# Expert stages of a two-block transformer: the first block's transposed rows as a product with a one-hot of positions

## The reference

```
def hier_moe(xf, w_rg, b_rg, w_re, b_re, w1, w3, w2):      # T rows of 1024
    ...                                  # router: best group of 4, in it the 2 best of 8 experts
    expert = g_idx * EXPERTS_PER_GROUP + top_i             # two experts for each token
    gate = jax.nn.softmax(top_v, axis=-1) * g_val
    ...                                  # the rows are sorted by expert and padded to blocks
    def expert_block(args):
        xblk, e = args
        return (jax.nn.silu(xblk @ w1[e]) * (xblk @ w3[e])) @ w2[e]
    yb = lax.map(expert_block, (xb, block_exp)).reshape(R, D)
    out = jnp.zeros((T + 1, D), yb.dtype).at[row_tok].add(yb * row_gate[:, None])
    return out[:T]
```

## Time and profile before

| | us |
|---|---|
| median of 3 runs (lowest, highest) | 2503.63 (2503.33, 2508.33) |
| the profiled execution | 2508.48 |
| its span | 2506.6 |
| PE busy in the span | 2295.7 (92%) |
| DVE, ACT, POOL busy | 1279.3, 689.4, 120.4 |

### The profile page before, as it was taken

The page is one execution under the profiler, slowest core; times in us unless marked ns, Lnnn a source line. Parts: engine busy times, 40 slices in busy tenths (PEclk is TensorE's granted clock), DMA queues, the critical chain, the costliest instruction groups (busy, mean ns, idle before and its releaser), DMA issues.

```text
span 2506.6 us, 37162 instructions
## 1 busy us (share of the span) xinstructions
PE 2295.7 (92%) x14742; PEld 1606.3 (64%) x14742; DVE 1279.3 (51%) x2026; ACT 689.4 (28%) x941; POOL 120.4 (5%) x219
## 2 busy tenths in 40 slices
PE   8999999989999999999948999999888779988887
PEld 7888788889888788888743444433485634333333
DVE  5556655565556655562564665555678532111112
ACT  4334543343334543342211011000146301100110
POOL 1000100000001000000001000000000010000000
PEclk9999999999999999999978999999989889999999
DMA  9774437757765287743267999999931479999997
GB/s 329 250 255 148 146 125 262 258 163 245 246 233 167 76 284 245 257 131 101 77 244 286 404 406 408 407 407 408 355 114 51 163 315 409 413 411 412 415 417 308
DMA packets 235391, 673.59 MB, mean 269 GB/s; under 512 B 23920, under 2 KB 163456, under 8 KB 181888
## 3 DMA queue, kind: packets, MB, share of 16 engines
q1 hardware_dynamic: 213584, 642.82, 68.6%
q0 software_dynamic: 9584, 17.52, 2.4%
q10 hardware_dynamic: 12096, 11.48, 1.5%
HBM read 675.62 MB, written 4.29 MB: 271 GB/s over the span
## 4 chain that ended last, share of the span: by engine, by line
PE 68%; DMA 19%; DVE 7%; DVEq 2%; ACT 2%; issue 2%; SPq 0%; ACTq 0%; POOLq 0%
PE ps L708 14%; PE ps L709 14%; PE ps L710 13%; DMA raw<-in_w 12%; PE ps L1155 11%; DMA expert_ahead<-in_w 7%; PE ps L1173 4%; PE ps L1226 2%; PE ps L722 2%; PE ps L749 2%; DVE w_lo L1912 1%; PE ps L1148 1%; DMA router_rows<-work 1%; PE ps L1165 1%; PE ps L1366 1%
## 5 line engine op out<-in xcount | busy, mean ns | idle before, releaser
L1912 DVE TENSOR_TENSOR w_lo<-raw,w_hi 128x2048 fp32r<-128x2048 f32 x180 | 411.1, 2289 | 318.0 <-ACT w_hi L1416 317.4
L708 PE MATMUL ps<-t_hi,w_hi 128*128 128x256 f32 (+1 forms) x1568 | 454.4, 290 | 0.1
L709 PE MATMUL ps<-t_lo,w_hi 128*128 128x256 f32 (+1 forms) x1568 | 452.6, 289 | 0.0
L1416 ACT CAST w_hi<-raw 128x2048 fp32r<-128x2048 f32 x180 | 342.1, 1905 | 394.9 <-PE ps L710 381.3
L710 PE MATMUL ps<-t_hi,w_lo 128*128 128x256 f32 (+1 forms) x1568 | 449.7, 287 | 0.0
L708 PE MATMUL ps<-w_hi,t_hi 128*128 128x256 f32 (+1 forms) x1088 | 352.2, 324 | 10.1 <-DVE t_lo L1912 7.9
L709 PE MATMUL ps<-w_lo,t_hi 128*128 128x256 f32 (+1 forms) x1088 | 351.3, 323 | 0.0
L710 PE MATMUL ps<-w_hi,t_lo 128*128 128x256 f32 (+1 forms) x1088 | 351.2, 323 | 0.0
L708 PEld LDWEIGHTS ps<-t_hi,w_hi 128*128 128x128 f32 x1568 | 295.0, 188 | 20.1 <-issue 13.2
L2624 DVE SCALAR_TENSOR_TENSOR work<-ps,work 128x512 f32<-128x512 f32 x64 | 48.1, 751 | 501.1 <-PE ps L1173 501.0
L710 PEld LDWEIGHTS ps<-t_hi,w_lo 128*128 128x128 f32 x1568 | 296.0, 189 | 4.6
(11 more groups left out here) (352 smaller groups left out, 2563.8 us busy)
## 6 DMA issues: line engine op xcount, KB each, us to landing
expert_ahead<-in_w SPq DMA_DIRECT2D x188, 1024.0 KB, 24.3
raw<-in_w SPq DMA_DIRECT2D x128, 1024.0 KB, 24.1
work<-in_w SPq DMA_DIRECT2D x60, 1024.0 KB, 26.4
work<-in_w_mod SPq DMA_DIRECT2D x32, 1536.0 KB, 6.5
raw<-in_ffn_w_gate SPq DMA_DIRECT2D x44, 1024.0 KB, 8.9
raw<-in_ffn_w_up SPq DMA_DIRECT2D x44, 1024.0 KB, 10.6
raw<-in_ffn_w_down SPq DMA_DIRECT2D x44, 1024.0 KB, 4.9
raw<-in_w_in SPq DMA_DIRECT2D x18, 1024.0 KB, 5.3
```

The lines of the kernel that those rows point to most:

```text
L708: pe.matmul(dst, a[0], b[0], start=start, stop=False)
L709: pe.matmul(dst, a[0], b[1], start=False, stop=False)
L1416: act.copy(slot(j)[0], src).then_inc(w_hi_ready, 1)
L1912: return dve.tensor_tensor(dst, src, hi.bitcast(F32), ALU.subtract)
```

## The change

For block 0 of each stage the rows are no longer gathered from DRAM and transposed. DVE makes a one-hot of position within expert 0 for every token (`r_first`), and PE multiplies the normed rows in SBUF with it (`first_rows`): the product is the transposed block. It goes to the same bank and through the same copy to `xT`, which moves to another place in the work area, since `hrow` still fills the old one when m = 0.

The main table (block = expert, 32 columns) is made at once, from positions alone. The spare blocks are worked out after it, and their columns come with the second table. Gather 0 is gone; gather 1 is the first. Gathers with a fixed block number read their addresses from `table` directly, with no copy and no drain. For m = 0, ACT's first copy to `gusb` now also waits for `h_stored`.

```
-                slot_table(1, 2)
-                pe.wait_ge(table_ready, m + 1)
+                def first_rows():
+                    pe.wait_ge(first_ready, m + 1)
+                    pe.wait_ge(rows_ready, TILES[0] * m + nt)
+                    for kk in range(KD):
+                        for t in range(nt):
+                            mm = pe.matmul(ps[:, 0, kk * BLK:(kk + 1) * BLK], hrow[:, t, :].rearrange("p (c k) -> p k c", k=KD)[:, kk, :],
+                                           r_first[:, t, :], start=t == 0, stop=t == nt - 1)
+                    mm.then_inc(xgt_ready, 1)
+
+                first_rows()
+                slot_table(1, 2, r_main_onehot, EXPERTS)
...
-                turn_rows(0, 0)
                 up_of(0, 0)
                 turn_rows(1, 1)
-                slot_table(2, 4)
+                pe.wait_ge(table_ready, m + 1)
+                slot_table(2, 4, r_onehot, nb + EXTRA[m])
                 turn_up(0, 0)
...
                 dve.wait_ge(pos_ready, m + 1)
+                pos_ps = ps[:, 1, 0:nt * 32].rearrange("p (t n) -> p t n", t=nt)
+                first = r_first[:, 0:nt, :]
+                wide = lambda v: v.to_broadcast([P, nt, BLK])
+                dve.tensor_tensor(first, iota[:, 0:BLK].unsqueeze(1).to_broadcast([P, nt, BLK]), wide(pos_ps[:, :, 0:1]), ALU.is_equal)
+                dve.drain()
+                dve.tensor_tensor(first, first, wide(r_mem[:, 0:nt, 0:1]), ALU.mult)
+                dve.drain().then_inc(first_ready, 1)
...
+                dve.tensor_tensor(blocks[:, :, :, 0:EXPERTS], r_oh[:, :, 0:nt, :], bk(tokid[:, :, 0:nt], EXPERTS), ALU.mult)
...
+                dve.tensor_tensor(chosen, r_oh[:, :, 0:nt, :], pos_ps.unsqueeze(1).to_broadcast([P, 2, nt, EXPERTS]), ALU.mult)
+                dve.drain()
+                dve.tensor_reduce(r_pos[:, :, 0:nt], chosen, X, ALU.add)
+                dve.drain()
+                dve.tensor_tensor(main, slots, bk(r_pos[:, :, 0:nt], BLK), ALU.is_equal)
+                dve.drain().then_inc(onehot_ready, 1)
+
+                dve.wait_ge(tps_ready, 2 * m + 1)
+                dve.tensor_scalar(table[0:BLK, 0:EXPERTS], ps[0:BLK, 2, 0:EXPERTS], 1.0, 4.0 * BANK, ALU.mult, ALU.add)
+                dve.tensor_scalar(token_f[:, 0:EXPERTS], ps[:, 2, 0:EXPERTS], 1.0, 4.0 * BANK, ALU.mult, ALU.add)
+                dve.drain().then_inc(table_ready, 1)
+
                 more = r_more[:, :, 0:2 * nt - 1]
...
-                for par in range(2):
-                    dve.wait_ge(xg_landed[m][par], 16)
-                block_onehots(gates)
+                onehots = r_onehot[:, 0:2 * nt, :].rearrange("p (k t) n -> p k t n", k=2)
+                is_blk = r_is_blk[:, 0:2 * nt, 0:nb].rearrange("p (k t) n -> p k t n", k=2)
+                dve.tensor_tensor(onehots, slots, bk(r_inf[:, :, 0:nt], BLK), ALU.is_equal)
...
+                dve.tensor_tensor(blocks[:, :, :, 0:nb], is_blk, bk(gates[:, :, 0:nt], nb), ALU.mult)
+                dve.tensor_tensor(blocks[:, :, :, nb:nb + nx], is_blk[:, :, :, EXPERTS:nb], bk(tokid[:, :, 0:nt], nx), ALU.mult)
+                dve.drain().then_inc(onehot_ready, 1)
...
+                    if isinstance(b, int):
+                        rows = table[0:BLK, b:b + 1]
...
-                gather(0, 0, True)
                 gather(1, 1, True)
```

More of the change, by code:

```diff
@@ L350, in build @@
         r_more = r(2592, EXPERTS, 7)
-        r_blk = r(2816, 8, 48)
+        r_blk = r(2816, 8, 64)
+        r_is_blk = r(1952, 8, 48)
+        r_pos = w(R2 + 2576, 8).rearrange("p (k t) -> p k t", k=2)
+        r_main_onehot = r(1440, 8, BLK)
+        r_first = w(R1 + 1040, 4 * BLK).rearrange("p (t n) -> p t n", t=4)
         r_onehot = r(256, 8, BLK)
@@ L455, in build @@
         onehot_ready = sem("slot_onehots_ready")
+        first_ready = sem("first_block_onehot_ready")
         tps_ready = sem("table_product_ready")
@@ L1135, in slot_table @@
                         for half in range(2):
[L1136 removed]
+                            mm = pe.matmul(ps[BLK * half:BLK * half + BLK, bank, 0:n], onehot[:, i, :], r_blk[:, i, 0:n],
                                            start=i == 0, stop=i == 2 * nt - 1)
                     mm.then_inc(tps_ready, 1)
[L1140 to L1141 removed]
+                def first_rows():
[8 more added lines that the diff above has]
+                slot_table(1, 2, r_main_onehot, EXPERTS)
                 def turn(par):
@@ L1770, in up_copy @@
                     act.wait_ge(expert_done, MAIN * m + (6 * b + 2 if not isinstance(b, int) or b else 4))
+                    if m == 0 and isinstance(b, int) and b == 0:
+                        act.wait_ge(h_stored, 64)
                     act.copy(gusb[:, par, :], ps[:, 1, :]).then_inc(gu_ready, 1)
@@ L2498, in moe @@
                 dve.wait_ge(pos_ready, m + 1)
+                pos_ps = ps[:, 1, 0:nt * 32].rearrange("p (t n) -> p t n", t=nt)
[5 more added lines that the diff above has]
+                dve.drain().then_inc(first_ready, 1)
                 pos = r_tmp[:, 0:nt, :]
-                dve.tensor_copy(pos, ps[:, 1, 0:nt * 32].rearrange("p (t n) -> p t n", t=nt))
+                dve.tensor_copy(pos, pos_ps)
                 dve.tensor_copy(r_cnt, ps[:, 1, nt * 32:nt * 32 + 32])
-                dve.drain()
+                tokid = k("tokid").rearrange("p (k t) -> p k t", k=2)
+                blocks = r_blk[:, 0:2 * nt, :].rearrange("p (k t) n -> p k t n", k=2)
+                bk = lambda v, n: v.unsqueeze(3).to_broadcast([P, 2, nt, n])
+                dve.tensor_tensor(blocks[:, :, :, 0:EXPERTS], r_oh[:, :, 0:nt, :], bk(tokid[:, :, 0:nt], EXPERTS), ALU.mult)
+                chosen = r_chosen[:, :, 0:nt, :]
+                main = r_main_onehot[:, 0:2 * nt, :].rearrange("p (k t) n -> p k t n", k=2)
+                slots = iota[:, 0:BLK].unsqueeze(1).unsqueeze(1).to_broadcast([P, 2, nt, BLK])
+                dve.tensor_tensor(chosen, r_oh[:, :, 0:nt, :], pos_ps.unsqueeze(1).to_broadcast([P, 2, nt, EXPERTS]), ALU.mult)
+                dve.drain()
+                dve.tensor_reduce(r_pos[:, :, 0:nt], chosen, X, ALU.add)
[6 more added lines that the diff above has]
+                dve.drain().then_inc(table_ready, 1)
                 more = r_more[:, :, 0:2 * nt - 1]
@@ L2542, in moe @@
                 dve.drain()
-                tokid = k("tokid").rearrange("p (k t) -> p k t", k=2)
-                def block_onehots(value):
-                    for kk in range(2):
-                        for t in range(nt):
-                            dve.tensor_scalar(r_blk[:, kk * nt + t, 0:nb], iota[:, 0:nb], r_blkf[:, kk, t:t + 1],
-                                              value[:, kk, t:t + 1], ALU.is_equal, ALU.mult)
-                    dve.drain().then_inc(onehot_ready, 1)
-                onehots = r_onehot[:, 0:2 * nt, :].rearrange("p (k t) n -> p k t n", k=2)
-                dve.tensor_tensor(onehots, iota[:, 0:BLK].unsqueeze(1).unsqueeze(1).to_broadcast([P, 2, nt, BLK]),
-                                  r_inf[:, :, 0:nt].unsqueeze(3).to_broadcast([P, 2, nt, BLK]), ALU.is_equal)
-                block_onehots(tokid)
                 dve.wait_ge(route_exp_ready, 2 * m + 1)
@@ L2588, in moe @@
                 dve.tensor_copy(extra_used[0:1, m:m + 1], incl[0:1, EXPERTS - 1:EXPERTS])
+                dve.wait_ge(tps_ready, 2 * m + 2)
+                dve.tensor_scalar(table[0:BLK, EXPERTS:nb], ps[0:BLK, 4, nb:nb + nx], 1.0, 4.0 * BANK, ALU.mult, ALU.add)
+                dve.tensor_scalar(token_f[:, EXPERTS:nb], ps[:, 4, nb:nb + nx], 1.0, 4.0 * BANK, ALU.mult, ALU.add)
                 dve.drain().then_inc(extra_ready, 1)
@@ L2823, in rows_in @@
                 def rows_in(b, par):
-                    pool.tensor_copy(table_col[0:BLK, par:par + 1], table[0:BLK, bass.ds(b, 1)])
-                    pool.drain()
+                    if isinstance(b, int):
+                        rows = table[0:BLK, b:b + 1]
+                    else:
+                        rows = table_col[0:BLK, par:par + 1]
+                        pool.tensor_copy(rows, table[0:BLK, bass.ds(b, 1)])
+                        pool.drain()
                     return pool.indirect_dma_start(out=xg[0:BLK, par, :], out_offset=None, in_=h_dram,
-                                                   in_offset=bass.IndirectOffsetOnAxis(ap=table_col[0:BLK, par:par + 1], axis=0),
+                                                   in_offset=bass.IndirectOffsetOnAxis(ap=rows, axis=0),
                                                    bounds_check=nt * P - 1, oob_is_err=False)
```

19 lines of the change are left out of this document (7 added, 12 removed).

## The result

| | us |
|---|---|
| median of 5 runs (lowest, highest) | 2489.3 (2488.61, 2493.57) |
| kernel before, median of 5 runs beside them | 2505.16 (2503.33, 2508.86) |
| ratio, 95% interval | 0.9938 (0.9923, 0.9952) |
| the profiled execution, its span | 2490.68, 2488.9 |

The changed kernel is 15.9 us faster (0.62%), inside the range of 2474 to 2492 and 7 us short of the forecast of 2482.

A forecast was written before the change was run, and what follows sets the result against it. Weights bound the long expert run, which could only start earlier, by as much as PE's work at the stage starts shrank. Gains of 8.8 (m = 0) and 12.5 us (m = 1), 21.3 together, gave a median of 2482, range 2474 to 2492.

The forecast's parts named there:

- The rule that the end moves by PE's work on blocks 1 to 3: Stage starts: the program's end moves as much as PE's work on these blocks, while DMA has a pause to give up.
- Rival 3: Stage starts: the head start is worth nothing because the weights bind and DMA regains its pause; 2503.6 us, chance 0.06.
- The new product at 0.12 a record: Block 0's one-hot product on PE: 64 records in 7.7 us for m = 0, 32 in 3.8 for m = 1.
- The clock rising during the product: PE, m = 0: dense work raises the clock after 3 to 4 us, so the first table takes 1.1 us, not 1.95.
- The hole of 7.2 us left with the first indirect transfer: POOL, m = 0: the one-time 7.2 us delay stays ahead of gather 1, which starts at about 1317.3.
- rival 2: POOL: the 7.2 us hole belongs to the copy and drain and falls on gather 2; 2475 us, chance 0.12.
- m = 1, 12.5 us forecast: Second stage start: block 1's up product ends at 2030.3 against 2042.85, with no PE idling and no clock lost.
- `h_stored` last in m = 0: Gather 1's release: the row store at 1309.58 comes after the table at 1309.4, so the store is last.
- DVE in time, DMA in time: Second one-hots ready 3.9 us before PE asks in m = 0; weight panels arrive before block 3 asks, so nothing eats the gain.
- rival 1: New product: loads and products don't overlap, 0.2 us a record, 12.8 and 6.4 us; 2490 us, chance 0.15.
- Rival 4: New product: records run unpipelined, only ground the accumulation in one place of PSUM; slower, 2516 us, chance 0.04.
- Rival 5: One stage's gain is halved by the clock in m = 1's block 0, late one-hots or slow gather 1; 2490 us, chance 0.07.

The follow-up runs named there:

- e8: Changed kernel with twelve extra matmuls ahead of the product to keep the clock up, and a plain contiguous stationary; 2479.9 us, 0.9898 of the kernel before.
- e12: Changed kernel with the extra clock-raising matmuls and a stationary stride of two elements (8 bytes) in place of eight; 2480.56 us (one time).
- e6: Changed kernel with eight extra matmuls while PE waited for the membership and four more ahead of the product, to raise the clock; 2491.2 us, 0.9948 of the kernel before.
- e11: Changed kernel with the extra clock-raising matmuls and both operands of the product cut to 64 partitions; 2494.59 us (one time).
- e9: Changed kernel with the extra clock-raising matmuls, product loops exchanged and no sums over the tiles; 2492.39 us (one time).
- e4: Changed kernel with the product's operands exchanged: one-hot stationary, rows moving 512 columns at a time, result then turned; 2478.39 us, 0.9894 of the kernel before.
- e1: Changed kernel with the product's stationary read from neighbouring columns in place of every eighth; 2489.23 us, 0.9938 of the kernel before.
- e3: Changed kernel with the copy of the table's column and the drain put back ahead of gather 1; 2500.95 us, 0.9982 of the kernel before.
- e5: Kernel before with only gathers 0 and 1 reading addresses directly from the table, no copy or drain; 2498.7 us, 0.9978 of the kernel before.
- e2: Changed kernel with the product for block 0 taking only the first tile of tokens, 16 records per stage; 2481.4 us, 0.9905 of the kernel before.

## Why the prediction was right or wrong

- **The rule that the end moves by PE's work on blocks 1 to 3**: right. Block 1's up product and SP's transfers moved by the same 8.3 us, and the weight-bound run kept its length. Over all the kernels the stage starts differ by up to 26.5 us, and what comes after them by 1.3. Rival 3 falls.
- **The new product at 0.12 a record: the step that failed.** It took the price from L1148, with the same stride and 64 moving columns. The product has 0.242 a record, 15.5 and 7.9 us for 7.7 and 3.8, above even the bound of 13.6, which came from a plain stationary at half clock. e8 and e12 show the forecast's size (0.124 and 0.127) once the stride is short and the clock up; e6 shows 0.24 with the long stride at full clock. The row of the right kind was L722, a float32 matmul like the new product: its 0.21 and 0.11 at half and full clock are what the plain product costs in e8 (0.213 and 0.112), and only the price of the stride was in no such row. Why the transposes of L1148 get by with 0.14 and less for one record of the same stride is open: hardly for their 64 partitions (e11), and not for having no sum (e9). They are one record for an operation of the code where a float32 matmul is two, and no run parts these. One row points the same way: the turning in e4 (L1164) is made of float32 matmuls with this stride, of 64 columns, on the two halves of the partitions side by side. Its 16 records for each half take 2.13 us, 0.13 each, which is about half of 0.24 for half the columns.
- **The clock rising during the product**: wrong. I took L722's dense work as the pattern; L1151 is as dense in the profile and the clock stayed at 0.50 for 15.3 us. The stride isn't the whole reason: in e1 the clock stayed at 0.50 too, for the 13.9 us of the plain product. Why it rose in L722 and in e4 and not here is open. So the first table (1.92 for 1.1 in m = 0) and the first 5 us of `up_of(0)`, in both stages, ran at half clock.
- **The hole of 7.2 us left with the first indirect transfer**: wrong. It follows the first copy (rival 2; e3, e5). The forecast read a hole of 8.05 us and later ones of 0.89; the two gathers between them had 2.79 and 2.50. Because the hole went elsewhere the errors nearly cancelled in m = 0, and that is luck. From start to start, the product was 7.7 us too long, the table 0.6 and `up_of(0)` 2.6, 10.9 together. Against it stand the 5.8 us of idling, the 2.0 of lost clock and 1.2 in the transposes, second table and `turn_up` that I had counted behind the late gather, 9.0 together. So 1.9 us were missing, and 2.0 were measured (6.8 for 8.8).
- **m = 1, 12.5 us forecast, 6.9 measured**: little there cancels. The product was 4.0 us too long from start to start, table and `up_of(0)` behind it 1.8, for the clock, and what follows 0.3 shorter than forecast: 5.5, where 5.6 are missing.
- **`h_stored` last in m = 0**: it would have been, had the product been short; e2 and e4 show gather 1 released by the store, at 1310.32 and 1309.99. In the changed kernel the table is last.
- **DVE in time, DMA in time**: right here. DVE's cover is thin, though: in the changed kernel of m = 0 its second one-hots are written at 1325.7 and PE comes to them at 1326.3, where the forecast had 3.9 us; e1 waits 0.28 us and e8 1.9. The landing of gather 1 among moving weights, forecast at 4.31, takes 6.69 and 7.78 in e2 and e3; in the changed kernel it landed before they restarted.
- **The rivals.** The size of the gain is that of rival 1 (a dearer record, 2490), not for its reason: a plain record costs 0.124 at full clock, under the 0.2 that a load and a product one after the other would need by that rival's sum. The rule of the Trainium skill, TensorE: Matmul & The Clock Gate, Part 3, The mechanism, that a load overlaps with running matmuls only when its row group differs, gave an estimate of 0.16 with that page's 107 ns for a load. The plain operand runs below it (0.124), so this trace doesn't bear the rule out; the strided one lies above it (0.24). Rival 2 was right in mechanism, but its 2475 needed a short product; e4 comes within 4 us of it. Rival 4's ground, the sums in one place, is ruled out by e9. Rival 5 has the size too (2490), and the clock in block 0 of m = 1, one of its grounds, did cost there, but the product cost more. The Trainium skill, GPSIMD Engine Reference, 2.1 Instruction dispatch, has about 6 us for the first call of a freshly loaded kernel: the runs have 8.05 us, 7.2 more than in the later rows of 0.89, behind the first copy with its drain, whichever gather that is. Whether it is such a load, and whether the copy or the drain brings it, no run shows.

## What to carry to other kernels

Before pricing a stream of small matmuls, look at the stride of the stationary operand; here a record with 32 bytes from column to column cost 0.24 us at either clock, where a plain one cost 0.21 at half and 0.11 at full. 8 bytes cost next to nothing, and exchanging the operands (few records, long moving rows) removed the question. Take the price from a row with the same kind of operation, not only the same shape: here a transpose was no measure for a matmul. And when a change moves a gather, ask what else the DMA engines will be doing then. When a part that looks like tidying stands in a change, run it alone: taking away the copy and drain ahead of the first gathers brought 5.5 us alone, the product alone 3.9, and both 15.9.

## What the runs showed of the hardware that was not expected

- Records of a float32 matmul, 128 stationary and 64 moving columns: 0.24 us with a stride of 32 bytes, whether the clock is at 0.50 (changed kernel, 0.242) or 0.94 (a stretch of e6); without stride 0.217 at half clock (e1) and 0.124 with the clock mostly at full (e8; from start to start 0.213 and 0.112 at the two clocks). With 8 bytes it is 0.127 (e12).
- The clock stayed at 0.50 through 15.3 us in which PE and its loads were busy throughout (changed kernel), and fell from 0.94 to 0.50 inside such a stream (e6). With the plain operand it stayed at 1.00 once it was up (e8), and at 0.50 where it was not, for 13.9 us (e1). A busy PE in the profile doesn't say that the clock will rise or stay.
- The hole behind GpSimd's first copy (8.05 us, for 0.89 in the kernel before from its fourth gather on) moves with that copy. An indirect transfer that reads its addresses directly has none, even as the first of the program (changed kernel and e5).
- Indirect transfers behind the first copy have holes too: 6.96 us at gather 3 and 8.14 at gather 4 in the changed kernel, where the kernel before had 0.89 at gather 3. It is not the full DMA alone, since from 1364 us on, at a share of 1.01, they are 0.9 again. Nothing waited for them, and their cause wasn't tried.
- A gather of 64 rows lands in 2.9 us with the DMA engines at a share of 0.14 (changed kernel), in 6.69 at 0.74 (e2) and in 7.78 at 1.02 (e3).
